# Strassen's scheme for all eight gates of the last branch, the first pair right behind the second branch's last output

## The reference, cut to what matters

```python
projected = jnp.einsum('bsnc,ncd->bsnd', branches, w_branch[l])
gates = jax.nn.sigmoid(gate_logits.reshape(B, S, N_BRANCH, D_MODEL))
merged = jnp.sum(gates * projected, axis=2)
x = x + rmsnorm(merged @ w_out[l], norm_mix_post[l])
```

## Time and profile before

| | |
|---|---|
| time, median of 3 runs | 1727.93 us (1727.89 to 1727.94) |
| the profiled execution's own time | 1727.82 us |
| its span, first to last instruction | 1726.0 us |
| TensorE busy, share of the span | 1710.7 us, 99% |
| DVE, ACT, POOL busy | 55%, 37%, 67% |

### The profile page before, as it was taken

How to read it: one execution, slowest core, us unless ns; L and a number is a source line. 1 busy time by engine, 2 the same in 40 slices (tenths; PEclk the granted TensorE clock), 3 DMA queues, 4 the chain that set the end, 5 groups by cost and what they waited for, 6 DMA issues and landing times.

```text
span 1726.0 us, 25879 instructions
## 1 busy us (share of the span) xinstructions
PE 1710.7 (99%) x9579; PEld 1445.1 (84%) x9579; DVE 945.9 (55%) x1666; ACT 637.7 (37%) x1281; POOL 1155.9 (67%) x1213
## 2 busy tenths in 40 slices
PE   8999999999999999999999999999999999999999
PEld 5786778899899888888888888777898888998997
DVE  6347666764165246544035474544755569772753
ACT  3236673355066113332105253455520223450542
POOL 6643567957646887657786776545479598577574
PEclk9999999999999999999999999999999999999999
DMA  6620013323323325222332222221243232224232
GB/s 230 209 77 28 22 55 99 108 98 105 115 74 108 111 76 183 71 89 93 101 98 85 74 86 79 72 72 64 79 147 107 84 98 93 104 87 135 74 111 73
DMA packets 48828, 167.14 MB, mean 97 GB/s; under 512 B 5678, under 2 KB 8814, under 8 KB 48320
## 3 DMA queue, kind: packets, MB, share of 16 engines
q1 hardware_dynamic: 47208, 160.22, 28.4%
q10 hardware_dynamic: 1496, 5.27, 0.9%
HBM read 160.34 MB, written 4.21 MB: 95 GB/s over the span
## 4 chain that ended last, share of the span: by engine, by line
PE 94%; DVE 3%; issue 2%; ACT 1%; DMA 0%; SPq 0%; DVEq 0%; ACTq 0%
PE bank L1042 92%; PE bank L1446 1%; PE bank L1492 1%; DMA x_sb<-in_x 0%; DVE sq_sum L2335 0%; DVE h_lo L2638 0%; DVE att_l_t L3129 0%; DVE att_l_t L3132 0%; ACT h_hi L2011 0%; DVE tmp L2970 0%; DVE o_lo L2319 0%; DVE tmp L3193 0%; DVE o_hi L2318 0%; PE bank L1608 0%; DVE att_l_t L3123 0%
## 5 line engine op out<-in xcount | busy, mean ns | idle before, releaser
L3333 POOL TENSOR_TENSOR w_lo_t<-w_raw,w_hi_t 128x256 fp32r<-128x256 f32 (+1 forms) x782 | 676.7, 895 | 21.0 <-ACT w_hi_t L1812 3.7
L3328 POOL TENSOR_SCALAR w_hi_t<-w_raw 128x1024 fp32r<-128x1024 f32 (+1 forms) x207 | 234.5, 1133 | 344.1 <-PE bank L1042 307.8
L1042 PE MATMUL bank<-h_hi,w_hi_t 128*128 128x512 f32 (+1 forms) x1172 | 421.8, 360 | 7.9 <-ACT h_hi L2011 7.9
L1042 PE MATMUL bank<-h_hi,w_lo_t 128*128 128x512 f32 (+1 forms) x1172 | 412.4, 352 | 0.0
L1042 PE MATMUL bank<-h_lo,w_hi_t 128*128 128x512 f32 (+1 forms) x1172 | 408.9, 351 | 0.3 <-DVE h_lo L2638 0.3
L1042 PEld LDWEIGHTS bank<-h_hi,w_hi_t 128*128 128x128 f32 x1172 | 222.9, 190 | 47.7 <-issue 18.6
L1042 PEld LDWEIGHTS bank<-h_lo,w_hi_t 128*128 128x128 f32 x1172 | 221.8, 189 | 30.6 <-DVE h_lo L2638 1.2
L1042 PEld LDWEIGHTS bank<-h_hi,w_lo_t 128*128 128x128 f32 x1172 | 223.0, 190 | 28.8 <-issue 1.2
L3254 POOL TENSOR_TENSOR w_lo_t<-w_raw,w_hi_t 128x512 fp32r<-128x512 f32 x76 | 98.8, 1299 | 124.3 <-ACT w_hi_t L1806 124.3
L1042 PE MATMUL bank<-hid_hi,w_hi_t 128*128 128x512 f32 (+1 forms) x439 | 170.1, 388 | 0.0
L1042 PE MATMUL bank<-hid_lo,w_hi_t 128*128 128x512 f32 (+1 forms) x439 | 169.5, 386 | 0.0
(11 more groups left out here) (481 smaller groups left out, 3275.2 us busy)
## 6 DMA issues: line engine op xcount, KB each, us to landing
w_raw<-in_w SPq DMA_DIRECT2D x259, 512.0 KB, 3.5
w_more<-in_w SPq DMA_DIRECT2D x17, 512.0 KB, 3.6
y<-in_w SPq DMA_DIRECT2D x6, 512.0 KB, 5.2
x_sb<-in_x SPq DMA_DIRECT2D x4, 512.0 KB, 7.4
park<-x_sb SPq DMA_DIRECT2D x4, 512.0 KB, 5.1
out_y<-x_sb SPq DMA_DIRECT2D x8, 256.0 KB, 2.3
x_sb<-in_x ACTq DMA_DIRECT2D x1, 1536.0 KB, 6.7
x_sb<-park ACTq DMA_DIRECT2D x1, 1536.0 KB, 8.9
```

What stands on the lines that cost most here:

```text
L1042: return pe.matmul(out, lhs, rhs, start=start, stop=stop, **kw)
L3328: pool.tensor_scalar(hi[:, 0:cols], src[:, 0:cols], 1.0, 0.0, ALU.mult, ALU.add).then_inc(*did("w_hi", i))
L3333: ins = pool.tensor_tensor(lo[:, piece], src[:, piece], hi.bitcast(F32)[:, piece], ALU.subtract)
```

## The change

`G_ALONE`, the number of gates of branch 2 that run alone, goes from 2 to 0, so that gates 0 and 1 become a fourth pair, the first of the phase. The preparation `st_pre` moves ahead, from behind br 1,7 to right behind swa_pv 7,1. `swa_split` stays where it was.

```diff
@@ -45,7 +45,7 @@
-G_ALONE = 2
+G_ALONE = 0
@@ -336,7 +336,8 @@
-    run([("st_pre", ("pair3", 0, G_ALONE)), ("swa_split", 0)] + [F(("gate", 2, m)) for m in range(G_ALONE)])
+    order.append(("swa_split", 0))
+    order.insert(order.index(("swa_pv", 7, 1)) + 1, ("st_pre", ("pair3", 0, G_ALONE)))
     for m in range(G_ALONE, KD, 2):
         lin(("pair3", 0, m), "pair", 2)
@@ -1874,6 +1875,7 @@
         def gates_phase(pairs):
+            functions("sigmoid")
             raw_hi(pairs[0], Q_W12)
             sum_hi(pairs[0], 4)
             act.wait_ge(*after("o_ready", 2, 0))
```

## The result

The changed kernel takes 1739.0 us (1737.99 to 1739.74, 6 runs) against 1727.91 (1727.57 to 1727.97, 6 runs): ratio 1.0064, 95% interval 1.0051 to 1.0077, 11.1 us slower. The forecast had 1736.6, with a range to 1738.3. The profiled execution took 1739.56, its span 1737.8.

A forecast was written before the change was run, and what follows sets the result against it. TensorE, busy 99% of the span, was taken as the bound. 1727.93 - 0.82 (matmuls) + 7.45 (wait for `u2_t`) + 0.1 (restart) + 2.0 (clock) = 1736.7, rounded 1736.6 us; range 1733.4 to 1738.3.

The forecast's parts named there:

- What bounds, and that the wait would come: TensorE's stream bounds the kernel; at W12 of the first pair it waits 7.45 us for DVE's `u2_t`.
- the queue that the forecast added up: DVE's four queued pieces from 1229.33 to the first pair's `u2_t`, together 17.53 us, done at 1246.86.
- Matmuls, -0.82: On TensorE, 48 matmuls of 512 columns (10.89 us) go and 84 of 256 (10.07 us) come: -0.82 us.
- Loads, banks, ACT: First pair's preparation: loads land by about 1222, banks are free in time, ACT keeps up; loads cost 0.
- eight `o_lo`: 1241.13 to 1246.06, 4.93 us: Piece of DVE's queue ahead of the first `u2_t`, priced at 4.93 us from the profile before.
- the 7.45: TensorE's wait at W12 of the first pair, from 1239.41 until `u2_t` at 1246.86: 7.45 us.
- POOL's low part of W12 takes 1.30: First pair's preparation on POOL: 1.30 us, ready by about 1242, before `u2_t`.
- the two pieces ahead of it: DVE's queue before `o_lo`: four sums with three low parts, 5.76 us; evacuations of br 1,6 and br 1,7, 2.98 us.
- Clock, 2.0 within 0 to 2.7: Behind TensorE's wait, matmuls restart at the lower clock: 2.0 us lost, from ten slow matmuls at program start; bounds 0 to 2.7.
- the forecast's upper bound: Clock loss behind the wait at most half of the 5.5 us slow stretch at program start: 2.7 us.
- Range: Whole kernel: 1733.4 to 1738.3 us, covering the wait with and without clock loss, plus DVE's queue error and clock bounds.
- the rival's 1734.6: Wait at W12 as worked out but the clock stays up behind it: 1734.6 us, chance 0.31.

The follow-up runs named there:

- `pool_later`: Changed kernel, but POOL's low parts of W12 and W22 of the first pair wait until the last `o_lo` is done; 1736.83 us, ratio 1.005.
- `spread`: Changed kernel with only two `o_lo` left ahead of the phase and two given to each pair on DVE; 1733.25 us, ratio 1.0031.
- `full_spread`: `spread` plus first-pair sums before T4's split, three second-pair sums before br 1,7's evacuation, ACT's W12 and S4 high parts before `o_hi`; 1728.24 us.
- `fill60`: Changed kernel with 60 additional matmuls, results thrown away, on TensorE before the one waiting for `u2_t`; 1736.33 us, ratio 1.0048.
- `full_spread2`: `full_spread` with first-pair `u2_t` ahead of the next pair's fourth sum and each pair's second `o_lo` one operation later; 1727.77 us, ratio 0.9998.
- `both_terms2`: `pool_later` plus 45 additional matmuls on TensorE, placed ahead of its wait for W12's low part; 1734.01 us, ratio 1.0036.
- `fill30`: Changed kernel with 30 additional matmuls, results thrown away, on TensorE before the one waiting for `u2_t`; 1738.16 us, ratio 1.0058.
- `pair_only`: Changed kernel with the fourth pair formed but `st_pre` left at its old place behind br 1,7; 1741.61 us, ratio 1.0076.
- `move_only`: Changed kernel with the two lone gates kept, so that only `st_pre` is moved ahead; 1735.2 us, ratio 1.004.
- `both_terms`: `pool_later` plus 45 additional matmuls on TensorE, placed behind its wait for W12's low part; 1739.61 us, ratio 1.0067.

## Why the prediction was right in its kind and off in its size

- **What bounds, and that the wait would come: right.** TensorE waits once, at W12 of the first pair, for DVE's `u2_t`; the chain names the queue that the forecast added up; pairs two to four show no wait. `pool_later`, `spread` and `full_spread` shorten that queue and the time follows.
- **Matmuls, -0.82: right.** 40.31 us of phase, with the wait of 9.13, the restart and the 2.57 of `fill60`, give 52.15 where 52.25 was measured; `full_spread2`, with its three short delays, comes to 40.94.
- **Loads, banks, ACT: right.** First sum at 1229.93, right behind the split of T4; ACT's `o_hi` were ahead of `o_lo` as worked out, and POOL's low part of W12 was there at 1241.43.
- **The failed step: "eight `o_lo`: 1241.13 to 1246.06, 4.93 us" as part of the 7.45.** It was mis-sized: 6.97 us measured. The price came from a row in which POOL's only instruction nearby (1240.08 for 1.30 us) overlapped the first `o_lo` by a quarter of a microsecond, and cost it 0.11 us unnoticed; in the new order the low parts of both W12 and W22 fall into the eight. Each costs one `o_lo` 1.07 us. `pool_later` takes this away: its row of eight is 4.90 us long where the changed kernel's is 7.04. The forecast priced POOL's work as time for POOL alone ("POOL's low part of W12 takes 1.30") and did not ask what runs beside it. The wait became 9.13 instead of 7.45: +2.04 for `o_lo`, -0.26 for the two pieces ahead of it, -0.10 because the first pair began 0.70 later than in the execution before and the queue 0.60 later.
- **Clock, 2.0 within 0 to 2.7: right in kind, low in size.** 2.57 by `fill60`. The ten slow matmuls at the start of the program, from which it was priced, did not fill their stretch: TensorE waited once more there, 0.38 us until 9.96. Behind the new wait it was busy all of the 5.9 us from 1249.38 to 1255.27, for which the forecast's upper bound, half of a busy stretch, was the nearer price. Why a slow stretch is as long as it is stays open. That the start of the program ran at the lower level, though the view prints 1.00 there, fits what the wait shows: at a granted 0.50 matmuls of 256 columns start 0.213 us apart, half of the 0.43 for 512 there.
- Sum by what was measured: 1727.91 - 0.82 + 9.13 + 0.14 + 2.57 = 1738.9, against 1739.0. The prediction's own sum is 1736.66. With its wait alone put right (+1.68) it would be 1738.34, just at the top of the range; the clock's 0.57 took the time past it.
- **Range.** Its top added 1.0 us for DVE's queue (6% of 17.5). The queue's true error was 1.8 (2.04 - 0.26), from one mechanism and not from spread over 25 operations. (At the bottom 1.2 was taken off where the text has 1.0; nothing hangs on it.) `both_terms2`, in which neither term is mis-sized, falls to 1734.0, 0.6 under the rival's 1734.6.

## What to carry to other kernels

Before replacing slow but independent work by faster work, see whose cover it was: here 10.9 us of lone gates hid a queue of 17.5 us on another engine, and 0.8 us of gain was paid with 11. When a queue is moved, lay the other engines' new times beside it: an instruction that takes both its inputs from SBUF had a different price beside GpSimd. A wait of TensorE costs its length and the slow matmuls behind it, and the second part cannot be scaled from the first: 13 behind 4.57 us, 22 behind 6.98, but 23 behind the 3.98 left in `fill30`.

## What the runs showed of the hardware

- **DVE and POOL.** DVE's `tensor_tensor` with both inputs in SBUF is held by a POOL `tensor_tensor` until that has ended: 1.75 us instead of 0.68 (`o_lo`), 1.66 instead of 0.69 (`bank<-w_raw` in `spread`); in `pair_only` the same sum took 1.75. In the kernel before, the changed kernel, `move_only`, `pair_only` and `spread` such an instruction ends 0.54 to 0.56 us after POOL's. A `tensor_scalar` of POOL (`w_hi_t<-w_raw`) does the same: in `move_only` the sum at 1229.76 lasted 1.54 us and ended 0.55 after it. DVE's instructions with one input in PSUM kept 0.68 to 0.70 beside POOL. It also goes the other way: where DVE's instruction had begun first, POOL's took up to 1.81 instead of 1.27 to 1.31, and only 1.34 where little of DVE's was left (0.21 us, `spread`). The kernel before has it too, where it costs nothing: POOL's low part at 1246.21 lasts 1.69 us, begun inside DVE's sum of 1246.06 to 1246.75. The Trainium skill, SBUF — State Buffer, section "Who interferes with whom", says that a DVE instruction with two SBUF inputs contends with a GpSimd instruction that reads SBUF, one with at most one such input does not; it calls the port pair that they share an exclusive lock, and has the order of issue decide who blocks. These rows agree with it in each of those cases.
- **The clock.** The granted clock came down to 0.50 with waits of 9.12, 6.98, 4.60 (`move_only`) and 4.57 us and with the 3.98 left in `fill30`. Behind them stood 27, 22, 13, 13 and 23 matmuls at 1.2 GHz; behind the 5.8 and 5.2 of `pair_only` 12 and 18, behind the 4.82 of `both_terms` 14. The count does not follow the length alone. Waits of 1.21 and 1.22 us left it at 1.00. That the clock falls again in a kernel in full run was open in the forecast; these rows show it, and agree with the Trainium skill, TensorE: Matmul & The Clock Gate, section "Why this matters for your kernels", that long gaps between bursts of matmuls bring the clock back to half.
- **A fill keeps the clock up only if it begins before the clock has fallen.** In `both_terms` 45 matmuls begun after 4.82 us of idle time took 7.10 us, the first 14 of them slow; in `both_terms2` they began without such a wait and took 5.66.
